# Order of work in the front of a transformer-block kernel: weight panels' low parts and heads' scalings placed anew

## The reference

```
u  = cols + mu_prev * (prev(cols) - cols) + mu_next * (next(cols) - cols)   # RWKV channels, shift over tokens
kv = rms_norm(c_kv) @ w_ukv      # per head: 64 of k, 64 of v
q  = rms_norm(c_q) @ w_uq        # per head: 64 + 32 (rope)
k_nope, q_nope, q_rope = rms_norm over each head, rope on the last
gates = sigmoid(gate_cols + b_gate)
```

## Time and profile before

| | us |
|---|---|
| median of 3 runs (lowest, highest) | 3369.89 (3364.22, 3376.41) |
| the profiled execution | 3384.76 |
| its span from first to last instruction | 3382.9 |
| PE busy in the span | 3193.5 (94%) |
| DVE busy | 2035.6 (60%) |
| ACT busy | 1068.7 (32%) |
| POOL busy | 315.4 (9%) |

### The profile page before, as it was taken

The page is one execution under the profiler, slowest core; times in us unless marked ns, Lnnn a source line. Parts: engine busy times, 40 slices in busy tenths (PEclk is TensorE's granted clock), DMA queues, the critical chain, the costliest instruction groups (busy, mean ns, idle before and its releaser), DMA issues.

```text
span 3382.9 us, 52078 instructions
## 1 busy us (share of the span) xinstructions
PE 3193.5 (94%) x22004; PEld 2545.1 (75%) x22004; DVE 2035.6 (60%) x3235; ACT 1068.7 (32%) x1526; POOL 315.4 (9%) x307
## 2 busy tenths in 40 slices
PE   8999998788988888999999999999998999999999
PEld 7777786576766767778888888877746888778887
DVE  4665454577777775534544444448979987655445
ACT  5222334444444442221111111122153333433332
POOL 0222342000000000401000000000000000000000
PEclk9999999789999998999999999999999999999999
DMA  3342666234344433421111111111101222213222
GB/s 143 118 137 68 220 209 202 62 83 100 83 105 98 95 66 136 149 93 38 50 50 50 50 50 44 44 38 42 46 13 50 99 89 99 87 69 129 90 99 75
DMA packets 93527, 301.86 MB, mean 89 GB/s; under 512 B 10352, under 2 KB 38640, under 8 KB 70768
## 3 DMA queue, kind: packets, MB, share of 16 engines
q1 hardware_dynamic: 79104, 246.63, 23.5%
q0 software_dynamic: 14192, 51.91, 4.5%
HBM read 241.35 MB, written 57.15 MB: 88 GB/s over the span
## 4 chain that ended last, share of the span: by engine, by line
PE 78%; DVE 11%; issue 3%; ACT 3%; DMA 3%; POOL 2%; SPq 1%; DVEq 0%; ACTq 0%; POOLq 0%
PE ps L2414 24%; PE ps L308 20%; PE ps L503 6%; PE ps L1755 3%; PE ps L2239 2%; PE ps L2556 2%; PE ps L1766 1%; PE ps L2074 1%; PE ps L1778 1%; PE ps L475 1%; DVE Yh L2583 1%; PE ps L1423 1%; PE ps L1019 1%; DMA Dn<-nbs 1%; PE ps L2434 1%
## 5 line engine op out<-in xcount | busy, mean ns | idle before, releaser
L2414 PE MATMUL ps<-Hh,whi 128*128 128x512 f32 x1600 | 498.4, 393 | 0.0
L284 ACT ACTIVATE whi<-raw 128x2048 fp32r<-128x2048 f32 x139 | 265.7, 1911 | 638.3 <-PE ps L308 310.4
L288 DVE TENSOR_TENSOR wlo<-raw,whi 128x2048 fp32r<-128x2048 f32 x139 | 319.0, 2295 | 132.9 <-ACT whi L284 132.7
L2414 PEld LDWEIGHTS ps<-Hh,whi 128*128 128x128 f32 x1600 | 300.5, 188 | 68.0 <-issue 6.2
L2414 PE MATMUL ps<-Hh,wlo 128*128 128x512 f32 x800 | 311.6, 390 | 0.0
L2414 PE MATMUL ps<-aHh,whi 128*128 128x512 f32 x512 | 200.0, 391 | 3.6 <-DVE xT L2760 2.5
L308 PE MATMUL ps<-Hhi,wlo 128*128 128x512 f32 x656 | 202.2, 389 | 0.0
L308 PE MATMUL ps<-Hhi,whi 128*128 128x512 f32 x656 | 202.1, 389 | 0.0
L308 PE MATMUL ps<-Hlo,whi 128*128 128x512 f32 x656 | 202.1, 389 | 0.0
L2414 PE MATMUL ps<-aHh,wlo 128*128 128x512 f32 x512 | 199.4, 389 | 0.0
L2414 PE MATMUL ps<-aLh,whi 128*128 128x512 f32 x512 | 199.4, 389 | 0.0
(11 more groups left out here) (385 smaller groups left out, 6199.9 us busy)
## 6 DMA issues: line engine op xcount, KB each, us to landing
raw<-in_panels SPq DMA_DIRECT2D x139, 1024.0 KB, 4.7
rwf<-F POOLq DMA_DIRECT2D x16, 1280.0 KB, 6.8
L<-rwf SPq DMA_DIRECT2D x16, 1024.0 KB, 5.0
L<-rwf SPq DMA_DIRECT2D x64, 256.0 KB, 4.1
Dn<-nbs SPq DMA_DIRECT2D x128, 128.0 KB, 5.4
gts<-so POOLq DMA_DIRECT2D x16, 512.0 KB, 3.2
gl<-gts SPq DMA_DIRECT2D x32, 256.0 KB, 3.6
rwt<-so POOLq DMA_DIRECT2D x15, 512.0 KB, 3.0
```

The costliest lines, as they stand in the source:

```text
L284: e.activation(whi[i % 2][:, :], raw_of(i)[:, :], AF.Copy).then_inc(*a_hi.up(i))
L288: e.tensor_tensor(wlo[i % 2][:, :], raw_of(i)[:, :], whi[i % 2][:, :].bitcast(F32), OP.subtract).then_inc(*v_lo.up(i))
L2414: m = e.matmul(ap, W[wi][:, kc, n0:n0 + 128], mov[mi][:, kc, :], start=x == 0 and q == 0, stop=x == len(kcs) - 1 and q == 2)
```

## The change

The low part of a panel becomes an item of its own in the list ("panel", key t + 1.31 where the channel is ready at t + 0.6), only on DVE and only for the RWKV channels; the panels of the gate channels stay inside `gt_dve`, and on ACT the high part stays inside "ready". The key of "out" goes from t + 1.2 to t + 0.8.

```diff
@@ rw_dve
         e.scalar_tensor_tensor(out=o[0:M, :], in0=ub[0:M, 2:S + 2], scalar=vec("mu_n", ch, 0, M), in1=o[0:M, :],
                                op0=OP.mult, op1=OP.add).then_inc(*v_rw.up("mix", ch))
+
+    def rw_panel_dve(e, ch):
+        pi, n0, M = RW[ch]
         if n0 == 128:
             panels_after(panel_dve, e, UIX[f"rw{pi}"])
@@ front
             if t % 2:
-                made.append((t + 0.6, "ready", t // 2))
+                made += [(t + 0.6, "ready", t // 2), (t + 1.31, "panel", t // 2)]
         for s, t in enumerate(STEPS):
-            made += [(t + 0.5, "in", s), (t + 1.2, "out", s), (t + 2.8, "turn", s)]
+            made += [(t + 0.5, "in", s), (t + 0.8, "out", s), (t + 2.8, "turn", s)]
@@ front_dve
             if name == "ready":
                 rw_dve(e, i) if i < 16 else gt_dve(e, i - 16)
+            elif name == "panel" and i < 16:
+                rw_panel_dve(e, i)
             elif name == "krope":
```

## The result

The change takes the kernel from 3370.53 us (median of 14 runs, 3364.22 to 3383.74) to **3357.28 us** (14 runs, 3353.3 to 3364.58). The ratio is 0.9958 with a 95% interval of 0.9947 to 0.9969: 13.3 us, 0.4%. The forecast was 3355.8, 14.1 us less than the 3369.89 of the first three runs.

What follows compares the result with a forecast made beforehand. PE sets the front, so the change can win only its gaps (24.8 of 264 us) and clock lost behind them. Terms 2.2 + 3.4 + 1.2 + 2.55 + 4.8 = 14.15, say 14.1, off 3369.89: 3355.8 us, range 3344 to 3367.

Steps and rivals of the forecast that it cites:

- What sets the time: PE sets the front; from 346.6 to 548 us it is full, so front savings shift everything behind.
- "out" passes no "ready": In the sorted list t + 1.2 and t + 0.8 lie between the same two, so sums pass no channel's shift on DVE.
- in 0: PE's 2.28 us gap at step 0: low part and cT 0 exchanged on DVE, gap goes, 2.2 us saved.
- in 2: PE's 2.44 us gap at step 2: exchanges on DVE and POOL leave 0.65; with clock 3.4 us, bounds 1.8 and 3.5.
- in 6: PE's 1.91 us gap at step 6: POOL's power starts ahead of turn 4, 1.2 us saved, no clock term.
- in 11: PE's 4.47 us gap at step 11: falls to 2.27, saving 2.2 plus 0.35 of clock, bounds 2.2 and 2.9.
- in 13 to in 15: PE's gaps of 0.85, 2.86 and 3.47 us: first two go, last becomes about 4.0; together 4.8 us saved.
- First unit: PE's 5.3 us gap before the first unit, waiting for head steps and `lw`: shifts with step 15, gap stays.
- Given back later: Rival: moved panels push the next channel in the front, so 8.3 us stays, 3361.6 us; chance 0.25.
- More than the sum: Rival: the 2.27 us gap keeps the clock and in 15's gap shrinks; 18.5 us saved, 3351.4 us; chance 0.07.
- Slower by the scan's clock: Rival: the scan's short waits fall anew, each extra drop costs 1.7 us; with 18 more, 3386 us; chance 0.08.
- POOL's exchanges worth nothing: Rival: only DVE's exchanges count in the front; 9.2 us saved, 3360.7 us; shares the 0.25 of the first rival.

Runs made afterwards that it cites:

- the outs ahead: The change plus low parts 11 and 13 a channel later, turns earlier on ACT and POOL, out 10 and 14 before the next shift: 3354.28 us, ratio 0.9939.
- the panels alone: Only DVE's five exchanges made in the kernel before, POOL's and ACT's orders kept: 3368.39 us against 3375.14, ratio 0.9979.
- turn 0 first: The change with only the exchange of turn 0 and out 1 undone on POOL and ACT; one run, 3363.42 us against 3367.67 for the kernel before.
- the first exchange alone: The kernel before with only the first of DVE's five exchanges (cT 0 before panel 1); one run, 3366.63 us against 3367.67.
- the control: The kernel before the change, run again unchanged: 3373.99 us against 3375.14, ratio 1.0001.
- the change again: The change itself, unchanged, measured a second time against the kernel before: 3359.96 us against 3375.76, ratio 0.9957.

## Why the prediction was right, point by point

- *What sets the time.* That a shift of the front goes through the full stretch to the end held: 16.45 us at the first unit, 15.49 at the first attention product, 13.3 in the medians. Between those two the full stretch lost 1 us by the clock: the 10 us around the first unit's gap had a mean of 0.66, before 0.83.
- *"out" passes no "ready".* It held, and the outs ahead show that really passing one gained nothing at in 15 and lost 1.6 us at the first unit.
- *in 0: 2.2.* Measured 2.19, and 2.2 alone.
- *in 2: 3.4.* 1.82 of wait and 1.59 of clock, 3.41. That both exchanges are needed is shown by the panels alone and by turn 0 first (1.96 instead of 0.62). The clock part is luck in part: the first exchange alone had the full 2.44 us gap and no drop. And the rule behind it, that a gap of 2.28 us or less has no drop, was read from one profile and does not hold: other runs had drops behind gaps of 1.91, 1.98 and 2.24 us.
- *in 6: 1.2.* 1.36.
- *in 11: 2.55.* Up to turn 11 2.83: wait 2.15, clock 1.47 (no drop after 2.27 us), given back at turn 11 0.79. The second profile of the change had the drop behind the same 2.27 us, and against the control it still has 2.7 up to turn 11: as the prediction had it, turn 11 takes most of that term anyway.
- *in 13 to in 15: 4.8.* 4.69 from turn 11 on. Inside it the terms came otherwise: the 0.85 of in 13 was covered by a drop behind turn 11's 2.02 us gap (1.43 lost), in 14 brought 3.15, in 15 2.12. The start of in 15 came out right since DVE's chain sets it; its gap was 3.03 and not 4.0, because PE had come later.
- *First unit: nothing, a gap of about 5.3.* This was off by 1.97, and the gap was 3.32. Of the 1.97, 1.2 is the load of `lw` (from its issue to the unit's first product 7.9 us, before 9.1); with the control and the change again as the pair the first unit has 14.7 where in 15 has 14.5. The control's gap was 3.99, too. So it is the execution's, not the change's.
- *Rivals.* Given back later: only turn 11, 0.8 us. More than the sum: no. Slower by the scan's clock: the scan did not get slower (845.0 and 846.8 us beside 856.9 and 848.1). The prediction's sign for it, a scan clock other than 0.91, could not tell: it was 0.92 with the change and 0.93 in the unchanged control. POOL's exchanges worth nothing: no, turn 0 first lost 1.3 us, and the panels alone are 7.3 us behind the change at in 15.
- *A slip in the sum.* The bounds of the terms add up to 12.2 and 14.6, where the prediction has 12.2 and 15. Nothing hangs on it.

## What to carry to other kernels

Where engines walk a hand-made order, read which pairs a changed key really exchanges on each engine before pricing it: here the named effect did not exist on one engine and a good part of the gain came from a queue that the name does not mention. Put work that nobody awaits behind the short links of a chain on every engine that the chain crosses; in the traces DVE alone gave half. And price starts, not gaps: a gap is the difference of two times that both move, and my expectations for the gaps at in 14 and in 15 failed where the start of in 15 came out at the edge of its range.

## What the runs showed of the hardware

TensorE's granted clock after a gap is in part chance. For each gap in the front I read the mean clock of the 10 us from 1 us before it. In the twelve profiles no gap of up to 1.5 us had a drop (29 of them), each gap of 2.6 us and more had one (29), and of the 23 between 1.9 and 2.44 us, 11 had one and 12 had none, with the same code and the same gap: 2.44 us read 0.83 in both profiles of before and 1.00 in the first exchange alone; 2.27 us at in 11 read 1.00 in the first profile of the change and 0.83 in the second. The granted clock of the change's first profile around in 11 and turn 11 (gaps 2.27 and 2.02):

```profile
239.79:249.79 10.00, 7.73 (x37) 6.45 (x36) 6.21 (x14) 2.10 (x2) 4.18 (x3) 1.00 0.37 109
258.38:268.38 10.00, 7.98 (x34) 5.20 (x33) 3.84 (x11) 3.97 (x4) 5.01 (x4) 0.83 0.37 112
```

A drop that leaves a mean of 0.83 costs 1.4 to 1.6 us here by the starts behind it. Of the 29 gaps of 2.6 us and more, eleven read 0.66 to 0.74 (the shortest of them 3.18 us), and such a one can cost twice as much: 2.9 us behind in 11's 4.46 us gap in the control, 1.5 behind the same gap in the first profile of before. So two executions of one kernel can differ by 1.5 us at each such gap, and the scan, which is full of short waits, took 834 to 857 us.
